# Layer 0's first two gate/value pairs computed from x times gain, before the shift is known, in a two-layer decoder kernel

## The chip, the cores and the metric

The kernel runs on one core of a Trainium2 chip. The number that counts is the device time of one launch in microseconds; the median of 3 runs of the kernel before is 2507.43 us (2504.96 to 2507.67).

Engines are named as in the profile: PE is TensorE (matrix products; PEld its weight loads), DVE VectorE, ACT ScalarE, POOL GpSimd, SP SyncE, which only issues DMAs here (a trailing q, as in ACTq, is an engine's issue queue). "bank" is one of the 8 PSUM banks of 128x512 float32.

## What is computed

```
for l in range(2):                                  # DEPTH
    mod = silu(c) @ w_ada[l] + b_ada[l]             # 9 * 1024 values: shift, scale, gate of three sub-layers
    h = rmsnorm(x, norm_ffn1[l]) * (1 + sc1) + sh1  # x is 512 x 1024
    x = x + 0.5 * g1 * (silu(h @ Wgate) * (h @ Wvalue)) @ Wdown      # 1024 -> 2 x 2816 -> 1024
    h = rmsnorm(x, norm_mix[l]) * (1 + sc2) + sh2
    x = x + g2 * mixer(h)                           # retention and windowed attention, gated, w_out
    h = rmsnorm(x, norm_ffn2[l]) * (1 + sc3) + sh3
    x = x + 0.5 * g3 * (silu(h @ Wgate) * (h @ Wvalue)) @ Wdown
out = rmsnorm(x, final_norm)
```

All is float32. With gain = norm weight * (1 + scale) and r the reciprocal root mean square of a token, h @ W equals r * ((x * gain) @ W) + shift @ W. So a product can start on x * gain alone; r is multiplied in afterwards, and shift @ W, one number per output column, is added.

## The kernel before

Activations lie transposed: 8 tiles of 128 model dimensions by 512 tokens (KT = 8, T = 512, P = 128). Each float32 operand is split into a high part (fp32r) and a low remainder, and each product is three matmuls (L1600 hi*hi, L1601 lo*hi, L1602 hi*lo). A "unit" is 128 output columns: 8 tiles of 3 matmuls for an up projection, 11 of 3 for a down projection. A "pair" is two units: one gate column block (unit 0, `pA[0]`) and its value block (unit 1, `pA[1]`), or two output blocks. Units of the same number share one raw buffer, one `w_hi` and one `w_lo` buffer, so for each unit SP loads 512 KB (`load`, L365) once DVE has split the unit in that buffer before it, ACT writes the high part (`split_weights`, L568) once PE has finished that earlier unit, DVE writes the low part (L943, a subtraction), and only then PE may start. The order on each engine is the written order; semaphores join them (`lo_ready` counts low parts, `unit_done` units, `bank_free` freed banks).

A feed-forward network runs in two halves: 11 up pairs (`up`: ACT Silu of the gate bank L681, DVE product with the value bank L1121, ACT high part L688, DVE low part L1124), then 4 down pairs, whose results DVE adds to x (L1097).

The modulation vector is computed on the side, 256 columns at a time, in "jobs" (`ada_sum_job`, L953 to L967): ACT issues the two loads of a job's 1 MB, DVE makes 8 multiply-adds of 128x256, one 32x32 transpose and one reduction. In ffn1 one job follows each up and down pair in DVE's order. `fold_jobs` (L1653) on PE sums the parts of a group of jobs once `ada_part_done` has counted them, and `ada_store` (L974) on DVE adds the bias. Job groups are GATE, MIX, REST and NEXT (the next layer's shift and scale).

Before the first pair of layer 0, shift and scale of ffn1 are computed from 16 blocks of 512 KB (`first_block`): PE multiplies a part of the columns (`first_rows`, L1561), DVE the others (`first_sum`, L1270 and L1273). x is transposed on PE (L1575). DVE and ACT then make tile after tile: x * r (L1286), times gain (L781), plus shift, high part (L785), low part (L1336). Layer 1 and the other norms already use the other way (`first_pairs` on ACT and DVE, `deferred_pairs` on PE): scaled x first, GpSimd sums shift times weight out of the raw buffer (`shift_products`, L489 to L497), PE sums that over its rows (`shift_sums`, L1632).

## Time and profile before

| what | value |
|---|---|
| median of 3 runs | 2507.43 us (2504.96 to 2507.67) |
| the profiled execution's own time | 2506.7 us |
| its span on the core | 2504.9 us |
| PE busy | 2472.0 us, 99% |
| DVE, ACT, POOL busy | 1501.5 us, 872.2 us, 210.3 us |
| DMA | 307.31 MB, mean 123 GB/s |
| chain that ended last, by engine | PE 94%, DVE 2%, issue 1%, ACT 1% |

The profile is one execution. Its span starts 1.8 us short of the time of that execution; every time of a row is counted from the start of the span. A busy time of PE counts a matmul until its last row has left, so consecutive rows overlap: the pitch of their starts is what a matmul costs. In an idle note, "[0.16 <-DVE sb_w_lo L943]" says that the engine was idle 0.16 us and which instruction it waited for.

### The profile page before, as it was taken

Reading aid. Unit: us, or ns where it says so; the run is one execution under the profiler, and the core shown is the slowest. Engines: PE = TensorE matmul, PEld = TensorE weight load, DVE = VectorE, ACT = ScalarE, POOL = GpSimd, SP = SyncE. Lnnn points to the kernel's source line nnn. Section 1 sums busy time; section 2 is a strip of 40 time slices with the busy share of each in tenths; the row PEclk is TensorE's granted clock in tenths of the full one; section 3 lists DMA queues with packets and bytes.
Section 4 is the critical chain, followed back from the end, with each engine's and each line's share of the span. In section 5 each row is a group of like instructions: output and inputs, shape, how many; then the busy total and the mean of one; then the engine's idle time right before and its main releaser. Section 6 shows DMA issues by size and latency. Waiting matters only on the chain.

```text
span 2504.9 us, 35621 instructions
## 1 busy us (share of the span) xinstructions
PE 2472.0 (99%) x11468; PEld 2012.8 (80%) x11468; DVE 1501.5 (60%) x2297; ACT 872.2 (35%) x1326; POOL 210.3 (8%) x151
## 2 busy tenths in 40 slices
PE   7999999999999999999999999999999999999998
PEld 5888888877788878888878888887777888788887
DVE  5677778677643477533467677877775435633332
ACT  3222333555423343222332223345553323331332
POOL 0013002000000040000140000210100002200001
PEclk9999999999999999999999999999999999999999
DMA  6665664222134336433336656532222343333332
GB/s 246 195 188 173 187 181 148 86 66 59 53 92 133 94 91 196 140 101 100 102 97 198 186 174 197 165 116 78 59 59 65 95 134 93 88 106 88 96 105 80
DMA packets 488916, 307.31 MB, mean 123 GB/s; under 512 B 9000, under 2 KB 480376, under 8 KB 488184
## 3 DMA queue, kind: packets, MB, share of 16 engines
q1 hardware_dynamic: 420816, 238.73, 32.2%
q10 hardware_dynamic: 68008, 67.48, 8.5%
q8 instruction: 41, 0.67, 0.1%
q14 instruction: 51, 0.42, 0.1%
HBM read 299.89 MB, written 6.29 MB: 122 GB/s over the span
## 4 chain that ended last, share of the span: by engine, by line
PE 94%; DVE 2%; issue 1%; ACT 1%; DMA 0%; DVEq 0%; SPq 0%; ACTq 0%
PE ps_proj L1600 28%; PE ps_proj L1602 28%; PE ps_proj L1601 28%; PE ps_mid L1870 1%; PE ps_mid L1766 1%; PE ps_o L1787 1%; PE ps_mid L1817 1%; PE ps_mid L1819 1%; PE ps_mid L1818 1%; PE ps_mid L1774 1%; PE ps_mid L1862 1%; DMA sb_scratch<-in_x 0%; DVE sb_scratch L1017 0%; PE ps_small L1593 0%; ACT sb_w_hi L568 0%
## 5 line engine op out<-in xcount | busy, mean ns | idle before, releaser
L1600 PE MATMUL ps_proj<-sb_a_hi,sb_w_hi 128*128 128x512 f32 x1908 | 745.5, 391 | 2.2 <-ACT sb_scratch L681 1.7
L1602 PE MATMUL ps_proj<-sb_a_hi,sb_w_lo 128*128 128x512 f32 x1908 | 742.8, 389 | 0.0
L1601 PE MATMUL ps_proj<-sb_a_lo,sb_w_hi 128*128 128x512 f32 x1908 | 742.8, 389 | 0.0
L568 ACT ACTIVATE sb_w_hi<-sb_raw 128x1024 fp32r<-128x1024 f32 (+1 forms) x388 | 430.9, 1110 | 849.1 <-PE ps_proj L1602 816.2
L943 DVE TENSOR_TENSOR sb_w_lo<-sb_raw,sb_w_hi 128x1024 fp32r<-128x1024 f32 (+1 forms) x388 | 514.1, 1325 | 323.2 <-ACT sb_w_hi L568 315.4
L1600 PE MATMUL ps_proj<-sb_h_hi,sb_w_hi 128*128 128x512 f32 x1212 | 480.1, 396 | 6.0 <-DVE sb_h_lo L1025 3.9
L1602 PE MATMUL ps_proj<-sb_h_hi,sb_w_lo 128*128 128x512 f32 x1212 | 472.4, 390 | 0.0
L1601 PE MATMUL ps_proj<-sb_h_lo,sb_w_hi 128*128 128x512 f32 x1212 | 472.2, 390 | 0.0
L1600 PEld LDWEIGHTS ps_proj<-sb_a_hi,sb_w_hi 128*128 128x128 f32 x1908 | 358.5, 188 | 78.7 <-ACT sb_scratch L681 3.0
L1602 PEld LDWEIGHTS ps_proj<-sb_a_hi,sb_w_lo 128*128 128x128 f32 x1908 | 358.4, 188 | 74.6
L1601 PEld LDWEIGHTS ps_proj<-sb_a_lo,sb_w_hi 128*128 128x128 f32 x1908 | 358.6, 188 | 74.3 <-issue 0.5
L1600 PEld LDWEIGHTS ps_proj<-sb_h_hi,sb_w_hi 128*128 128x128 f32 x1212 | 227.6, 188 | 66.4 <-issue 14.0
L1602 PEld LDWEIGHTS ps_proj<-sb_h_hi,sb_w_lo 128*128 128x128 f32 x1212 | 227.6, 188 | 48.5
L1601 PEld LDWEIGHTS ps_proj<-sb_h_lo,sb_w_hi 128*128 128x128 f32 x1212 | 227.7, 188 | 45.3
L955 DVE SCALAR_TENSOR_TENSOR sb_scratch<-sb_scratch,sb_c_act 128x256 f32<-128x256 f32 x448 | 223.7, 499 | 16.1
L471 POOL TENSOR_TENSOR sb_scratch<-sb_scratch 128x512 f32<-128x512 f32 x36 | 61.3, 1702 | 1567.1 <-ACT sb_scratch L579 1567.1
L1097 DVE SCALAR_TENSOR_TENSOR sb_x_or_values<-ps_proj,sb_half_gate,sb_x_or_values 128x512 f32 (+1 forms) x80 | 60.0, 750 | 198.5 <-PE ps_proj L1602 196.9
L1121 DVE TENSOR_TENSOR sb_scratch<-sb_scratch,ps_proj 128x512 f32<-128x512 f32 x82 | 56.4, 688 | 173.7 <-PE ps_proj L1602 173.5
L681 ACT ACTIVATE sb_scratch<-ps_proj 128x512 f32<-128x512 f32 x82 | 49.0, 598 | 303.8 <-PE ps_proj L1602 303.8
L752 ACT ACTIVATE sb_scratch<-sb_scratch,sb_small 128x256 f32<-128x256 f32 x128 | 63.1, 495 | 0.0
L1010 DVE SCALAR_TENSOR_TENSOR sb_h_lo<-sb_x_or_values,sb_gain,sb_h_hi (+1 forms) x40 | 58.7, 1467 | 5.6 <-ACT sb_h_hi L614 5.0
L1124 DVE TENSOR_TENSOR sb_a_lo<-sb_scratch,sb_a_hi 128x512 f32 (+1 forms) x82 | 56.1, 684 | 0.0
(210 smaller groups left out, 1824.6 us busy)
## 6 DMA issues: line engine op xcount, KB each, us to landing
sb_raw<-in_ffn_w_up SPq DMA_DIRECT2D x176, 512.0 KB, 3.8
sb_scratch<-in_w_ada ACTq DMA_DIRECT2D x128, 512.0 KB, 4.2
sb_raw<-in_w_in SPq DMA_DIRECT2D x100, 512.0 KB, 3.8
sb_raw<-in_ffn_w_down SPq DMA_DIRECT2D x64, 704.0 KB, 4.5
sb_raw<-in_w_branch_swa SPq DMA_DIRECT2D x16, 512.0 KB, 3.6
sb_raw<-in_w_branch_ret SPq DMA_DIRECT2D x16, 512.0 KB, 3.6
sb_raw<-in_w_out SPq DMA_DIRECT2D x16, 512.0 KB, 3.5
sb_scratch<-in_w_ada SPq DMA_DIRECT2D x10, 512.0 KB, 7.4
```

What stands on the lines that cost most here:

```text
L471: pool.tensor_tensor(square_sum, square_sum, squares[:, k % 2, :], ALU.add).then_inc(sq_used, 1)
L568: act.activation(Whi[s][:, 0:n], raw[s][:, 0:n], ACT.Copy).then_inc(hi_ready, 1)
L752: last = act.activation(p, p, ACT.Exp, bias=neg_m[w][:, n:n + 1], scale=HD ** -0.5, accum_out=row_sum[w][:, n:n + 1])
L943: dve.tensor_tensor(Wlo[s][:, 0:n], raw[s][:, 0:n], Whi[s][:, 0:n].bitcast(F), ALU.subtract).then_inc(lo_ready, 1)
L955: ins = dve.scalar_tensor_tensor(ada_acc, ada_raw[s][:, k % 4, :], col, ada_acc, ALU.mult, ALU.add)
L1010: dve.scalar_tensor_tensor(Hlo[:, k, :], XV[:, k, :], gain[:, bass.ds(k, 1)], Hhi[:, k, :].bitcast(F), ALU.mult, ALU.subtract).then_inc(gx ...
L1097: dve.scalar_tensor_tensor(XV[:, m, :], pA[s][:, :], half_gate[:, bass.ds(m, 1)], XV[:, m, :], ALU.mult, ALU.add).then_inc(bank_free[s], 1)
L1121: dve.tensor_tensor(work, side, pA[1][:, :], ALU.mult).then_inc(bank_free[1], 1)
L1124: dve.tensor_tensor(Alo[:, i, :], work, Ahi[:, i, :].bitcast(F), ALU.subtract).then_inc(act_lo, 1)
L1600: pe.matmul(bank, Whi[s][:, w], hi, start=first, stop=False)
L1601: pe.matmul(bank, Whi[s][:, w], lo, start=False, stop=False)
L1602: return pe.matmul(bank, Wlo[s][:, w], hi, start=False, stop=last)
```

## The change

- Head of layer 0. x is loaded in 4 blocks of 128 tokens, each between two scale blocks, and transposed block by block. DVE no longer multiplies x by r there: ACT and DVE split x * gain (`scaled_hi`, `scaled_lo`) as soon as the scale is known. Pairs 0 and 1 run on that. The shift blocks (now wholly on DVE, 128x1024 each) are summed meanwhile. Pair 2 is the first on normalised and shifted tiles, by tile; pair 3 follows. The four pairs are written out ahead of the loop over layers.
- The shift columns of pair 0 are 16 one-column products on PE among the products of pair 2 (`kept_columns`), those of pair 1 are made by GpSimd after the last normalised tile and summed by PE in the middle of pair 3 (`kept_sums`). Both read the weights of these units from a second copy in SBUF, loaded again (`keep`, 4 loads of 512 KB).
- Jobs. Layer 0's job 0 comes after pair 3 instead of after pair 1, and each further job after one up pair later than before. In layer 1 too the jobs run one pair later. Half 0 of ffn1 now has 13 jobs instead of 14, and the last job of a layer runs after pair 2 of ffn2. GATE is 8 jobs instead of 9, MIX 16 instead of 15. The REST group is folded in ffn2 and not in the mixer's first pair; NEXT is folded after half 0's down pairs of ffn2, and its first job, which stood in half 1, runs with the others.

```diff
-SCALE_PE, SHIFT_PE, FIRST_BUFS = 6, 4, 9
-ACT_COPIES, FIRST_AHEAD = (5, 6, 7), 3
-HALF_JOBS = (JOBS - FIRST_JOBS) // 2
-GATE_JOBS, MIX_JOBS = HALF - 2, HALF + 4
+SCALE_PE, FIRST_BUFS = 4, 9
+HALF_JOBS = HALF + KT // 2 - 2
+GATE_JOBS, MIX_JOBS = HALF - 3, HALF + 5
...
+            for n in range(2 * KT):                                          # SP
+                if n < TT:
+                    sp.dma_start(xtok[:, n, :], x[0, P * n:P * (n + 1), :]).then_inc(x_in[n], 16)
+                if n == KT - 1:
+                    load(0, 0, up_v[0][0, 0, 0])
+                first_block(n)
+                if n == KT - 1:
+                    load(0, 1, up_v[0][0, 1, 0])
+                if n == KT + TT - 1:
+                    for s in range(2):
+                        load(1, s, up_v[0][0, s, 1])
...
+            keep(0)
+            for s in range(2):
+                load(2, s, up_v[0][0, s, 2])
+            keep(1)
...
+            pool.wait_ge(split_lo, KT)                                       # POOL
+            for s in range(2):
+                pool.wait_ge(kept_in[1][s], 16)
+                st.mark(pool.tensor_tensor(shift_tmp..., kept[1][s]..., shift, ALU.mult))
+                for n in (UP_UNIT // 2, UP_UNIT // 4):
+                    st.mark(pool.tensor_tensor(shift_tmp[:, 0:n], shift_tmp[:, 0:n], shift_tmp[:, n:2 * n], ALU.add))
+                pool.tensor_tensor(shift_acc[2 + s], shift_tmp[:, 0:P], shift_tmp[:, P:2 * P], ALU.add).then_inc(shift_made, 1)
...
+                hi(2, 3, 4, 5, 6, 7)                                         # ACT, end of the head
+                gate(0, 0)
+                split_weights(3, 0, UP_UNIT)
+                rest(0, 0)
+                split_weights(3, 1, UP_UNIT)
+                act.wait_ge(unit_done, 2 * 2 + 3)
+                act.wait_ge(bank_free[1], 2)
+                act.activation(side, pair_banks[2][0], ACT.Silu).then_inc(bank_free[0], 1)
+                rest(2, 1)
+                gate(1, 2)
+                rest(1, 2)
...
+            for k in range(KT):                                              # DVE
+                dve.wait_ge(gain_ready, 1)
+                scaled_lo(0, k)
+                if k == TT - 1:
+                    split_weights(0, 1, UP_UNIT)
...
+                def gate(p, turn):
+                    dve.wait_ge(shift_ps, p + 1)
+                    dve.tensor_copy(shift_col[:, 2 * p:2 * p + 2], first_sums[p]).then_inc(shift_cols, 1)
+                    dve.wait_ge(unit_done, 2 * p + 3)
+                    dve.wait_ge(act_lo, turn + 1)
+                    dve.tensor_tensor(work, pair_banks[p][0][:, :], rstd_row, ALU.mult).then_inc(scaled, 1)
...
+                lo(7)
+                gate(0, 0)
+                split_weights(3, 0, UP_UNIT)
+                value(0, 0)
+                rest(0, 0)
+                split_weights(3, 1, UP_UNIT)
...
+                dve.tensor_tensor(work, side, pair_banks[2][1], ALU.mult).then_inc(bank_free[1], 1)
+                rest(2, 1)
+                gate(1, 2)
+                value(1, 2)
+                rest(1, 2)
+                ada_sum_job(0, FIRST_JOBS, 0)
...
-                rest = FIRST_JOBS + GATE_JOBS + MIX_JOBS                     # DVE, mixer's first pair
-                ada_store(fold_no(l, REST_FOLD), rest, JOBS - rest, MOD_TILES * l + 2 * rest)
...
+                idle(pair_banks[1][0], 3)                                    # PE
+                for s in range(2):
+                    unit(0, 0, s, h_tile, waits={} if s else {k: (gx_lo, k + 1) for k in range(KT)})
+                unit(1, 1, 0, h_tile, ..., after={SPREAD_AT: lambda: spread_rstd(0, pO, 0).then_inc(rb_ready, 1)})
+                unit(1, 1, 1, h_tile, ..., after={KT - 2: shift_columns})
+                idle(pair_banks[2][0], 2)
...
+                unit(3, 3, 0, tile, freed=1)
+                unit(3, 3, 1, tile, freed=1, after={2: kept_sums})
```

In the three places below, rows name the line of the kernel they belong to, the operation, what is written and read, and the shape.

DVE, layer 0, from the splits of pair 3's weights to the first split of pair 4's, before. L943 is the low part of a weight unit (the digit is its buffer), L1121 and L1124 the product and low part of an up pair, L953 to L967 a job.

```order
L943 TENSOR_TENSOR sb_w_lo0<-sb_raw0,sb_w_hi0 128x1024
...
L953 TENSOR_SCALAR sb_scratch<-sb_scratch,sb_c_act 128x256
...
L967 TENSOR_REDUCE sb_scratch<-sb_scratch 128x8
L1144 UNCONDITIONAL_BRANCH
...
L1121 TENSOR_TENSOR sb_scratch<-sb_scratch,ps_proj1 128x512
...
L943 TENSOR_TENSOR sb_w_lo1<-sb_raw1,sb_w_hi1 128x1024
L1124 TENSOR_TENSOR sb_a_lo<-sb_scratch,sb_a_hi 128x512
```

The same stretch after the change, where L1009 is the low part of a weight unit, L1437 the product of pair 2, L1390 to L1405 the late work of pair 1, L1019 to L1033 the job, and L1206 the branch over layer 1's first pairs, behind which the first split of pair 4 stands.

```order
L1009 TENSOR_TENSOR sb_w_lo1<-sb_raw1,sb_w_hi1 128x1024
L1437 TENSOR_TENSOR sb_scratch<-sb_scratch,ps_mid 128x512
...
L1390 COPY sb_small<-ps_o 128x2
L1393 TENSOR_TENSOR sb_scratch<-ps_mid,sb_scratch 128x512
L1399 TENSOR_TENSOR sb_scratch<-ps_mid,sb_scratch 128x512
L1401 SCALAR_TENSOR_TENSOR sb_scratch<-sb_scratch,sb_small 128x512
L1405 TENSOR_TENSOR sb_a_lo<-sb_scratch,sb_a_hi 128x512
L1019 TENSOR_SCALAR sb_scratch<-sb_scratch,sb_c_act 128x256
L1021 SCALAR_TENSOR_TENSOR sb_scratch<-sb_scratch,sb_c_act 128x256 x7
L1031 STREAM_TRANSPOSE sb_scratch<-sb_scratch 128x256
L1033 TENSOR_REDUCE sb_ada_part<-sb_scratch 128x8
L1446 TENSOR_SCALAR sb_sinks<-sb_sinks 128x32
```

Between the last split of pair 3 and the first of pair 4 stood one up pair's two operations and one job; now the products of pairs 2 and 1 and a job stand there.

PE, layer 0, unit 1 of pair 3 and what follows, after the change: L1706 to L1708 are the three matmuls of a product (on `ps_proj1`), L1792 the two sums of `kept_sums`, L1928 and L1863 the entry of the loop over layers, behind which the skipped pairs of layer 1 and then pair 4 stand. Before, no such sum stood among the products of layer 0's pair 3.

```order
L1706 MATMUL ps_proj1<-sb_a_hi,sb_w_hi1 128x512
L1707 MATMUL ps_proj1<-sb_a_lo,sb_w_hi1 128x512
L1708 MATMUL ps_proj1<-sb_a_hi,sb_w_lo1 128x512
L1792 MATMUL ps_o<-sb_consts,sb_scratch 128x1 x2
L1706 MATMUL ps_proj1<-sb_a_hi,sb_w_hi1 128x512
...
L1928 UNCONDITIONAL_BRANCH
L1863 COMPARE_AND_BRANCH
```

What moved: the sums come after three of the eight tiles of that unit, and DVE's late work of pair 1 waits for them.

DVE, the mixer's first pair in both layers, before: L1017 scales a tile, L1025 is its low part, L1353 scales a unit's result, L974 is `ada_store` of the REST group (four rows of 32 partitions).

```order
L1025 SCALAR_TENSOR_TENSOR sb_h_lo<-sb_scratch,sb_mod,sb_h_hi 128x512
L1352 REGISTER_ALU
L1353 TENSOR_TENSOR sb_scratch<-ps_proj,sb_scratch 128x512
L974 ISA
L974 TENSOR_TENSOR sb_mod<-ps_mid,sb_vector_cols 32x8
...
L1017 SCALAR_TENSOR_TENSOR sb_scratch<-sb_scratch,sb_gain,sb_x_or_values 128x512
L1024 REGISTER_ALU
L1025 SCALAR_TENSOR_TENSOR sb_h_lo<-sb_scratch,sb_mod,sb_h_hi 128x512
```

After the change the four L974 rows and their registers are gone from this place; they stand at the end of ffn2's first up half.

## Rows read from the trace of the kernel before

**Rows 1.** Page, section 1, busy time, and section 2, PE's granted clock in 40 slices

```profile
PE 2472.0 (99%) x11468; PEld 2012.8 (80%) x11468; DVE 1501.5 (60%) x2297; ACT 872.2 (35%) x1326; POOL 210.3 (8%) x151
PEclk9999999999999999999999999999999999999999
```

**Rows 2.** PE's waits over the span: us in total, times, longest

```profile
PE ps_proj L1600 <- DVE sb_h_lo L1025: 3.9, 8, 0.8
PE ps_mid L1817 <- DVE sb_h_lo L1025: 2.0, 2, 1.0
```

**Rows 3.** Timeline of PE: start us, duration us, engine, line, operation, [idle before]

```profile
15.16 1.09 PE L1575 MATMUL ps_proj<-sb_consts,sb_scratch 128*128 128x128 f32 x8 [2.99 <-DMA sb_scratch<-in_x]
...
28.71 3.68 PE L1561 MATMUL ps_mid<-sb_scratch,sb_c_act 128*128 128x512 f32 x8
...
45.34 1.42 PE L1600 MATMUL ps_proj<-sb_a_hi,sb_w_hi 128*128 128x512 f32 x1
...
58.39 0.49 PE L1600 MATMUL ps_proj<-sb_a_hi,sb_w_hi 128*128 128x512 f32 x1 [0.34 <-DVE sb_w_lo L943]
...
91.47 0.49 PE L1600 MATMUL ps_proj<-sb_a_hi,sb_w_hi 128*128 128x512 f32 x1 [0.16 <-DVE sb_w_lo L943]
```

**Rows 4.** Timeline of ACT, head: weight splits that waited for their load

```profile
23.43 1.06 ACT L568 ACTIVATE sb_w_hi<-sb_raw 128x1024 fp32r<-128x1024 f32 x1 [2.15 <-DMA sb_raw<-in_ffn_w_up]
25.16 1.06 ACT L568 ACTIVATE sb_w_hi<-sb_raw 128x1024 fp32r<-128x1024 f32 x1 [0.68 <-DMA sb_raw<-in_ffn_w_up]
```

**Rows 5.** Timeline of DVE, head: operations of the scale columns and shift sum

```profile
24.06 0.48 DVE L1273 SCALAR_TENSOR_TENSOR sb_pos_i<-sb_consts,sb_c_act,sb_pos_i 128x256 f32<-128x256 f32 x1
...
29.61 0.95 DVE L1294 TENSOR_REDUCE sb_scratch<-sb_scratch 128x6 f32<-128x768 f32 x1
...
31.94 0.75 DVE L1273 SCALAR_TENSOR_TENSOR sb_scratch<-sb_scratch,sb_c_act 128x512 f32<-128x512 f32 x1
```

**Rows 6.** Groups of DVE and ACT by form: count, busy us, mean ns

```profile
L943 DVE TENSOR_TENSOR sb_w_lo<-sb_raw,sb_w_hi 128x1024 fp32r<-128x1024 f32 x324 | 407.9, 1259 | 285.6 <-ACT sb_w_hi L568 277.8 <-DVE sb_scratch L1219 0.5
L1121 DVE TENSOR_TENSOR sb_scratch<-sb_scratch,ps_proj 128x512 f32<-128x512 f32 x82 | 56.4, 688 | 173.7 <-PE ps_proj L1602 173.5
L1017 DVE SCALAR_TENSOR_TENSOR sb_scratch<-sb_scratch,sb_gain,sb_x_or_values 128x512 f32<-128x512 f32 x30 | 22.9, 764 | 0.1
L688 ACT ACTIVATE sb_a_hi<-sb_scratch 128x512 f32 x64 | 40.5, 633 | 1.1
L614 ACT ACTIVATE sb_h_hi<-sb_x_or_values,sb_gain 128x512 fp32r<-128x512 f32 x20 | 14.2, 710 | 5.0 <-DVE sb_gain L1004 5.0
```

**Rows 7.** Timeline of PE, layer 0's mixer: 8 one-column sums of two passes

```profile
410.10 1.84 PE L1593 MATMUL ps_small<-sb_consts,sb_scratch 128*128 128x1 f32 x16
```

**Rows 8.** Timeline of POOL, layer 0's ffn2: one unit's shift products

```profile
913.91 2.10 POOL L489 TENSOR_TENSOR sb_scratch<-sb_raw,sb_mod 128x1024 f32<-128x1024 f32 x1 [0.20 <-POOL sb_scratch L497]
916.18 1.51 POOL L494 TENSOR_TENSOR sb_scratch<-sb_scratch 128x512 f32<-128x512 f32 x1 [0.18 <-POOL sb_scratch L489]
917.88 1.50 POOL L494 TENSOR_TENSOR sb_scratch<-sb_scratch 128x256 f32<-128x256 f32 x1 [0.18 <-POOL sb_scratch L494]
919.87 0.56 POOL L497 TENSOR_TENSOR sb_scratch<-sb_scratch 128x128 f32<-128x128 f32 x1 [0.49 <-POOL sb_scratch L494]
```

**Rows 9.** Timeline of DVE in the same stretch

```profile
916.48 2.30 DVE L943 TENSOR_TENSOR sb_w_lo<-sb_raw,sb_w_hi 128x1024 fp32r<-128x1024 f32 x1
...
918.78 0.68 DVE L1041 TENSOR_TENSOR sb_scratch<-ps_proj,sb_scratch 128x512 f32<-128x512 f32 x1
```

**Rows 10.** Timeline of DVE, head: job 0 from first to last operation

```profile
77.26 0.34 DVE L953 TENSOR_SCALAR sb_scratch<-sb_scratch,sb_c_act 128x256 f32<-128x256 f32 x1
...
81.77 0.42 DVE L967 TENSOR_REDUCE sb_scratch<-sb_scratch 128x8 f32<-128x256 f32 x1
```

**Rows 11.** Stretches: length, busy time of PE, PEld, DVE, ACT, POOL, granted clock, DMA

```profile
39.00:42.00 3.00, 1.03 (x6) 1.03 (x6) 2.41 (x4) 0.00 (x0) 0.00 (x0) 0.86 0.39 82
42.00:45.00 3.00, 3.00 (x7) 1.71 (x7) 2.16 (x5) 2.06 (x4) 0.00 (x0) 0.50 0.93 377
45.00:48.00 3.00, 3.00 (x7) 1.83 (x6) 3.00 (x6) 2.94 (x5) 0.00 (x0) 0.50 0.50 160
48.00:51.00 3.00, 3.00 (x15) 2.48 (x14) 1.24 (x3) 0.00 (x0) 0.00 (x0) 1.00 0.92 269
```

**Rows 12.** Timeline, layer 0's ffn1, down pairs of half 1: PE's fold, DVE's job

```profile
355.04 0.38 PE L1653 MATMUL ps_mid<-sb_scratch,sb_consts 128*128 128x120 f32 x2
...
355.82 0.42 DVE L967 TENSOR_REDUCE sb_scratch<-sb_scratch 128x8 f32<-128x256 f32 x1
```

**Rows 13.** Timeline, mixer's first pair of layer 0: DVE's store, PE's second tile

```profile
422.09 0.68 DVE L974 TENSOR_TENSOR sb_mod<-ps_mid,sb_vector_cols 32x8 f32<-32x8 f32 x4
...
424.27 0.50 PE L1817 MATMUL ps_mid<-sb_w_hi,sb_h_hi 128*128 128x512 f32 x1 [0.99 <-DVE sb_h_lo L1025]
```

386 lines of the change are left out of this document (219 added, 167 removed).

## Prediction

> **What bounds the kernel now.** I read the page's busy times and PE's granted clock first. PE is busy 2472.0 of 2504.9 us at the full clock [rows 1], so only its holes or its work can move the time. The list of PE's waits comes second: its entries inside the layers are a few us (3.9 and 2.0 us are the largest two [rows 2]), so the stages behind the head have little to give. The timeline of PE comes third. Its first product starts at 45.3 us, pair 1 at 58.4 us, pair 4 at 91.5 us [rows 3]; from pair 1 to pair 4 that is 33.1 us for three pairs, 11.0 us each, which is 0.227 us per matmul (48 to a pair) with a hole of some tenths at two borders. So the head, up to 45.3 us, is what the change can earn from, and I follow it to the point where both kernels do the same again: the start of pair 4, 91.5 us before.
>
> **When pair 0 starts.** The bytes ahead of pair 0's second unit are the same as before (x, 8 scale blocks, 2 units), so it lands at 25.2 us as before; the last scale block and the first unit change places, and I put the block at the 23.4 us at which that unit landed [rows 4]. DVE then does the low part of unit 0 (1.2 us [rows 6], to 24.5), a copy (0.4), the last scale sum of 512 columns (0.75 us [rows 5], to 25.6), product with the identity and reduction of 512 columns (0.7 us each, scaled from 0.95 us for 768 [rows 5]) and three small adds: the gain is there at 27.4 us. ACT needs 0.71 us for the first tile, DVE 0.75 us [rows 6]. First product: 29.0 us. Before it PE has four filler matmuls, the last three at 0.9 us each at the full clock [rows 3] (the eight passes at 28.71 are four blocks), which end there too. Bounds: 27 us if the block lands 2 us earlier, 31.7 us if PE has the lower clock by then and its fillers take double.
>
> **PE from there to the middle of pair 3.** Pairs 0 to 2 and 11 of pair 3's 16 tile steps are 3.7 pairs of 10.9 us, 40.2 us. Added: spreading r 0.8, 8 + 16 one-column products at 0.21 us (8 take 1.7 us of pitch [rows 7]) 5.1, two filler matmuls 1.7, the two sums of pair 1's shift 0.4. Waits: 1.0 in pair 0, since DVE makes the tiles at 0.67 us each, PE's own pace, and stops once for a 1.2 us split; 2.0 at pair 2, where each tile costs DVE two operations of 0.75 us; 0.8 at pair 3, whose unit 0 can be split only when PE has left unit 0 of pair 2 (ACT 1.06 us [rows 4], then DVE). Sum 52.0 us: PE ends the sums of `kept_sums` at 81.0 us, and without any wait would end pair 3 at 84.4 us. Up to here it is 7 us ahead of before.
>
> GpSimd does not decide this by itself. Its four operations take 2.1 + 1.5 + 1.5 + 0.6 us and four gaps, 6.2 us per unit [rows 8], 12 us for both; the last tile is there at 65.5 us, so it ends near 78 us, 2 us before PE asks.
>
> **The wait that replaces the head's.** Pair 4's unit 0 waits for its low part, and DVE has all this before it: copy 0.15, gate of pair 1 times r 0.69, ACT's Silu 0.7, value times r 0.69, product 0.75, ACT's high part 0.63, low part 0.69 [rows 6], then job 0, 4.9 us from 77.26 to 82.19 [rows 10], sinks and loop entry 0.6, the split 1.2, and 0.2 of handing over. That is 11.2 us in a row from 81.0, no part of which can begin before PE's sums: pair 4 starts at 92.2 us. PE has 3.4 us of work for these 11.2, and stands still for 7.8. Before, job 0 lay under pair 2, where DVE had nothing else [rows 10]; now it is on the path. So pair 4 starts 0.7 us later than before, and the whole gain of the head is spent there. The later pairs have 8.7 us of DVE work (split 1.2 twice, 0.69 twice, a job 4.9) against 10.9 of PE, so the lag doesn't grow.
>
> **What the hole does to the clock.** Before, PE is idle 2 us near 39 to 41 us after a thin stretch, its granted clock falls within 39 to 42 and is 0.50, that is 1.2 GHz, until 48, though PE is busy all the time from 42 [rows 11]. 7.8 us of idleness is more than any hole in this trace before its last product. If the clock falls as it did there, the products behind run at half speed for up to (1 - 0.86) * 2 * 3 + 6 = 6.8 us, a loss of up to 3.4 us. Lower bound 0: the 2.99 us hole at 12 to 15 us left the clock full [rows 3]. I take 2.5, near the upper end, since this hole is nearer in kind to the one that cost. The Trainium skill, "TensorE: Matmul & The Clock Gate", Part 1, speaks against the change here: the slower clock is the default and only activity lifts it. By that rule the loss is certain; by the 2.99 us hole alone the sum would be 2.5 us less.
>
> **DVE beside GpSimd.** The low part of a unit takes 1.26 us on average [rows 6] and 2.30 us beside GpSimd, while a product that reads PSUM keeps 0.68 us [rows 9]. I charged pair 3's first split so (2.3 us); without it pair 4 would start 0.8 us earlier. The Trainium skill, "GPSIMD Engine Reference", section 1, says that the SBUF interfaces are shared with VectorE, with contention for instructions that have two SBUF inputs; the trace agrees. By a rule that slowed every DVE operation, the sum would be about 1 us more.
>
> **The rest of the program.** MIX is folded after the first unit of half 1's down pairs. Before, it needed 24 jobs of 25 done; now it needs 24 of 24, the last being the job of up pair 10. PE's fold starts at 355.04, that job ends at 356.24 [rows 12]: a new wait of 1.2 us in each layer, 2.4. REST: the store of 0.7 us leaves DVE ahead of the tile that PE waits 0.99 us for in the mixer's first pair [rows 13]: 0.7 less in each layer, 1.4. The folds cost PE the same where they now stand, and the job moved to ffn2 lies under products of 10.9 us. Bounds of this part: -1.4 (no new wait) to +2.4; I take +1.0, since both come from rows of the very places. The 2 MB loaded twice and SP's stop at `load(1, 1)` behind unit 1's split (32 us) put the last shift block at 41 us, and DVE needs it at 48, so I take 0, up to 1 us if the queue lands as slowly as its 9 us at worst.
>
> **Sum.** +0.7 + 2.5 + 1.0 = +4.2 us. The profiled execution took 2506.7 us, so 2510.9 for its like; the median of the runs is 0.7 above it, which gives 2511.6 us. Least: start at 27 (-2), no contention (-0.8), clock full (0), rest -1.4, so 0.7 - 4.2 = -3.5. Most: lower clock at pair 0 (+2.7), columns and GpSimd dearer (+1.1), clock 3.4, rest 2.0, so +9.9.
>
> **The rivals.**
> - The hole at pair 4 doesn't lower the clock: +1.7, 2509.1 us. For it the 2.99 us hole, against it the length. 13%.
> - The clock is already low when pair 0 starts, since PE has less to do in the head (512 instead of 768 columns per scale block): +2.7 on top, +6.9, 2514.3 us. For it the fall at 41 us in a similar thin stretch [rows 11], against it that 15 to 33 us stayed full. 20%.
> - The other side: DVE's chain isn't the bound, because pair 1's late work or the job finishes under pair 3. Then pair 4 starts at 84.4, 7.1 us early, and the clock holds: -7.1 + 1.0 = -6.1, 2501.3 us, faster. It decides if the chain behind the sums is under 3.4 us instead of 11.2. For it: DVE has a quarter of the time idle in the head; against it: the written order. 8%.
> - A weight unit or shift block lands so late that PE waits for loads in pairs 1 to 3: each us late is a us, from about 7 us behind my times on; with 2 us, 2513.6 us. 9%.
> - The forecast as summed: 50%.
>
> **Range and chances.** What a measurement of this kernel can tell from no change is about 0.2%, 5 us. The forecast lies at +4.2 with some 2 us of spread, so a third of its 50 lies beyond +5; with nearly all of the low-clock rival and half of the late loads that is 41% slower. Faster is the third rival, 7%; the same 52%. The range takes in both clock cases and the lower end of the sum to -3 : 2504.5 to 2516.5.
>
> **What the new profile would show.** PE's first product at 29 us; about 16 us for pair 2; one PE wait of 7 to 8 us for DVE's low part at the start of pair 4, near 84 to 92 us, the longest of the span; granted clock at 0.50 behind it for 3 to 7 us; the job directly ahead of that split on DVE; waits of 1.2 us before the MIX folds near 356 and 1582 us. I am wrong if pair 4 starts before 89 us, if the hole is under 4 us, or if the clock stays full.

## The result, and the profile after

The changed kernel takes 2514.71 us (median of 11 runs, 2513.42 to 2519.49) against 2506.87 us of the kernel before (11 runs beside them): ratio 1.0032, 95% interval 1.0023 to 1.0040, slower by some 8 us. The profiled execution took 2514.69 us, its span is 2512.9 us. The page's busy times, which answer to [rows 1]:

```profile
PE 2473.7 (98%) x11490; PEld 2014.3 (80%) x11490; DVE 1514.4 (60%) x2303; ACT 878.1 (35%) x1332; POOL 222.3 (9%) x159
```

PE is busy 1.7 us longer; the other 6 us of the longer span are holes. PE's waits over the span, against [rows 2]:

```profile
PE ps_proj L1706 <- DVE sb_w_lo L1009: 8.5, 1, 8.5
PE ps_proj L1706 <- DVE sb_h_lo L1091: 4.1, 8, 0.8
PE ps_mid L1758 <- DVE sb_ada_part L1033: 2.2, 2, 1.1
PE ps_mid L1950 <- DVE sb_h_lo L1091: 0.5, 2, 0.3
```

One wait of 8.5 us is new and the longest; two of 1.1 us at a fold are new; the two in the mixer went from 2.0 to 0.5 us. Where the first stands, in PE's timeline of the head (the first products of pairs 0, 2 and 4, and the sums of pair 1), against [rows 3]:

```profile
23.58 1.12 PE L1667 MATMUL ps_mid<-sb_scratch,sb_c_act 128*128 128x512 f32 x2 [1.94 <-DMA sb_scratch<-in_w_ada]
24.55 1.73 PE L1777 MATMUL ps_mid<-sb_x_or_values,sb_consts 128*128 128x512 f32 x2
26.07 1.71 PE L1771 MATMUL ps_small<-sb_consts,sb_scratch 128*128 128x1 f32 x8
27.64 4.76 PE L1777 MATMUL ps_mid<-sb_x_or_values,sb_consts 128*128 128x512 f32 x6
31.83 0.80 PE L1706 MATMUL ps_proj<-sb_h_hi,sb_w_hi 128*128 128x512 f32 x1
...
59.00 0.47 PE L1706 MATMUL ps_mid<-sb_a_hi,sb_w_hi 128*128 128x512 f32 x1 [0.37 <-DVE sb_a_lo L1091]
...
83.00 0.50 PE L1792 MATMUL ps_o<-sb_consts,sb_scratch 128*128 128x1 f32 x4
...
95.51 0.79 PE L1706 MATMUL ps_proj<-sb_a_hi,sb_w_hi 128*128 128x512 f32 x1 [8.47 <-DVE sb_w_lo L1009]
```

Pair 0 starts 13.5 us earlier than before (45.34), pair 4 starts 4.0 us later (91.47). The six passes of three filler products take 4.76 us, 0.8 us each (a filler is a product with the identity whose result nobody reads; each takes two passes). The stretches of the same profile show the clock (columns as in [rows 11]):

```profile
24.00:27.00 3.00, 3.00 (x10) 1.60 (x8) 2.75 (x5) 1.06 (x1) 0.00 (x0) 0.62 1.04 394
27.00:30.00 3.00, 3.00 (x7) 1.79 (x8) 1.55 (x6) 1.79 (x3) 0.00 (x0) 0.50 1.04 385
30.00:33.00 3.00, 3.00 (x8) 1.50 (x7) 3.00 (x5) 3.00 (x6) 0.00 (x0) 0.74 0.40 97
```

```profile
87.00:90.00 3.00, 0.05 (x1) 0.00 (x0) 2.53 (x6) 1.84 (x3) 0.00 (x0) 0.93 0.02 5
90.00:93.00 3.00, 0.00 (x0) 0.00 (x0) 2.77 (x7) 0.40 (x1) 0.00 (x0) 0.50 0.56 171
96.00:99.00 3.00, 3.00 (x8) 2.33 (x8) 2.90 (x5) 0.63 (x1) 0.00 (x0) 0.50 0.61 181
99.00:102.00 3.00, 3.00 (x13) 2.38 (x12) 2.81 (x6) 0.00 (x0) 0.00 (x0) 0.86 0.62 174
```

It is at 0.50, 1.2 GHz, twice: behind the wait of 1.94 us, until pair 0's first product, and in the hole before pair 4, until 99.5 us. What DVE does while PE stands still (timeline, from PE's sums of pair 1 to pair 4's first split):

```profile
83.61 0.69 DVE L1393 TENSOR_TENSOR sb_scratch<-ps_mid,sb_scratch 128x512 f32<-128x512 f32 x1
85.15 0.69 DVE L1399 TENSOR_TENSOR sb_scratch<-ps_mid,sb_scratch 128x512 f32<-128x512 f32 x1 [0.85 <-ACT sb_scratch L825]
85.88 0.75 DVE L1401 SCALAR_TENSOR_TENSOR sb_scratch<-sb_scratch,sb_small 128x512 f32<-128x512 f32 x1
87.33 0.69 DVE L1405 TENSOR_TENSOR sb_a_lo<-sb_scratch,sb_a_hi 128x512 fp32r<-128x512 f32 x1 [0.70 <-ACT sb_a_hi L829]
87.94 0.35 DVE L1019 TENSOR_SCALAR sb_scratch<-sb_scratch,sb_c_act 128x256 f32<-128x256 f32 x1
88.32 3.61 DVE L1021 SCALAR_TENSOR_TENSOR sb_scratch<-sb_scratch,sb_c_act 128x256 f32<-128x256 f32 x7
...
92.77 0.17 DVE L1446 TENSOR_SCALAR sb_sinks<-sb_sinks 128x32 f32<-128x32 f32 x1
94.11 1.22 DVE L1009 TENSOR_TENSOR sb_w_lo<-sb_raw,sb_w_hi 128x1024 fp32r<-128x1024 f32 x1 [1.16 <-ACT sb_w_hi L608]
```

Late work, job, sinks, the loop's entry, split: 12.0 us from the end of PE's sums (83.50) to pair 4. Its gaps are two waits for ACT inside pair 1's late work (0.85 and 0.70 us) and 1.16 us before the split. The profile puts this last one down to ACT, but ACT's high part of that unit had ended at 88.9 us; what stands there in DVE's order is the entry of the loop over layers. In run 8, where the split is no longer there, a gap of 1.20 us stands behind the same sinks and the profile puts it to "issue".

Followed through the program by PE's start times after minus before: pair 0 -13.5, pair 4 +4.0, the mixer's first pair +6.4 (424.27 to 430.63), layer 1 +6.8, its mixer +7.4 (1650.37 to 1657.75), end of the span +8.0 us.

### The profile page after: what moved, and what is told of

Same layout as the page of the kernel before. It is cut to its first block, busy times and chain, and to the rows that moved or that the text cites. A ratio compares the mean times of both kernels' runs of the same rounds, so it can differ in the third digit from the quotient of the medians.

```text
span 2512.9 us, 35648 instructions
## 1 busy us (share of the span) xinstructions
PE 2473.7 (98%) x11490; PEld 2014.3 (80%) x11490; DVE 1514.4 (60%) x2303; ACT 878.1 (35%) x1332; POOL 222.3 (9%) x159
## 4 chain that ended last, share of the span: by engine, by line
PE 91%; DVE 2%; issue 1%; ACT 1%; DVEq 0%; ACTq 0%
PE ps_proj L1706 27%; PE ps_proj L1708 27%; PE ps_proj L1707 27%; PE ps_mid L2003 1%; PE ps_mid L1903 1%; PE ps_o L1924 1%; PE ps_mid L1950 1%; PE ps_mid L1952 1%; PE ps_mid L1951 1%; PE ps_mid L1911 1%; PE ps_mid L1995 1%; ACT sb_w_hi L608 0%; DVE sb_scratch L1083 0%; PE ps_small L1699 0%; DVE sb_w_lo L1009 0%
## 5 line engine op out<-in xcount | busy, mean ns | idle before, releaser
L1706 PE MATMUL ps_proj<-sb_a_hi,sb_w_hi 128*128 128x512 f32 x1878 | 734.0, 391 | 10.2 <-DVE sb_w_lo L1009 8.5
L1708 PE MATMUL ps_proj<-sb_a_hi,sb_w_lo 128*128 128x512 f32 x1878 | 731.5, 390 | 0.0
L1707 PE MATMUL ps_proj<-sb_a_lo,sb_w_hi 128*128 128x512 f32 x1878 | 731.4, 389 | 0.0
L1009 DVE TENSOR_TENSOR sb_w_lo<-sb_raw,sb_w_hi 128x1024 fp32r<-128x1024 f32 (+1 forms) x388 | 514.2, 1325 | 319.2 <-ACT sb_w_hi L608 306.3
L1706 PE MATMUL ps_proj<-sb_h_hi,sb_w_hi 128*128 128x512 f32 x1210 | 479.7, 396 | 6.1 <-DVE sb_h_lo L1091 4.1
L1708 PE MATMUL ps_proj<-sb_h_hi,sb_w_lo 128*128 128x512 f32 x1210 | 471.6, 390 | 0.0
L1706 PEld LDWEIGHTS ps_proj<-sb_a_hi,sb_w_hi 128*128 128x128 f32 x1878 | 353.0, 188 | 85.5 <-issue 8.9
L1708 PEld LDWEIGHTS ps_proj<-sb_a_hi,sb_w_lo 128*128 128x128 f32 x1878 | 352.9, 188 | 73.8
L1707 PEld LDWEIGHTS ps_proj<-sb_a_lo,sb_w_hi 128*128 128x128 f32 x1878 | 353.2, 188 | 72.6
L1706 PEld LDWEIGHTS ps_proj<-sb_h_hi,sb_w_hi 128*128 128x128 f32 x1210 | 227.2, 188 | 66.9 <-issue 14.1
L1708 PEld LDWEIGHTS ps_proj<-sb_h_hi,sb_w_lo 128*128 128x128 f32 x1210 | 227.1, 188 | 48.5
L1076 DVE SCALAR_TENSOR_TENSOR sb_h_lo<-sb_x_or_values,sb_gain,sb_h_hi 128x512 fp32r<-128x512 f32 (+1 forms) x48 | 64.2, 1347 | 6.4 <-ACT sb_h_hi L649 6.2
L775 ACT ACTIVATE sb_scratch<-ps_proj 32x512 f32<-32x512 f32 (+1 forms) x48 | 28.4, 591 | 78.9 <-PE ps_proj L1708 78.6
```

Of the source, the lines that this page charges most:

```text
L1009: dve.tensor_tensor(Wlo[s][:, 0:n], raw[s][:, 0:n], Whi[s][:, 0:n].bitcast(F), ALU.subtract).then_inc(lo_ready, 1)
L1076: dve.scalar_tensor_tensor(Hlo[:, k, :], XV[:, k, :], gain[:, bass.ds(k, 1)], Hhi[:, k, :].bitcast(F), ALU.mult, ALU.subtract).then_inc(gx ...
L1706: pe.matmul(bank, Whi[s][:, w], hi, start=first, stop=False)
L1707: pe.matmul(bank, Whi[s][:, w], lo, start=False, stop=False)
L1708: return pe.matmul(bank, Wlo[s][:, w], hi, start=False, stop=last)
```

## The experiments

Each was timed against the kernel before; the "changed kernel" below is the one of this document, 2514.7 us.

**1. Most of job 0 left out.** Seven multiply-adds of job 0 are gone from DVE.

```diff
-                ada_sum_job(0, FIRST_JOBS, 0)
+                ins = dve.tensor_scalar(ada_acc, ada_raw[0][:, 0, :], c_act[:, 0:1], None, ALU.mult)
+                ...   # semaphores raised as the job does
+                dve.transpose(ada_turned, ada_acc).then_inc(ada_turn, 1)
+                dve.reduce_sum(ada_part[:, 0:8], ...).then_inc(ada_part_done, 1)
```

> Changed kernel; of job 0 only the first multiply, the transpose and the reduction are left on DVE, the seven multiply-adds (3.6 us) are left out, so 256 columns of the modulation vector are wrong. Theory A (DVE's row of work between the two sums of pair 1 and pair 4's first split sets pair 4's start): pair 4 starts 3.6 us earlier, at 91.9 instead of 95.5 us, the hole is 4.9 instead of 8.5 us, and the time falls by 3.6 us to 2511.1 us, or by up to 5.5 us to 2509.2 us if the shorter hole leaves the clock full. Rival B (the hole ends with the landing of pair 4's weights or with ACT's split): pair 4 starts within 0.5 us of 95.5, and the time stays at 2514.7 us within 1 us.

Measured: 2509.64 us (11 runs), ratio 1.0011 (1.0002 to 1.0020), 5.1 us less. PE's hole in its timeline:

```profile
96.64 0.79 PE L1715 MATMUL ps_proj<-sb_a_hi,sb_w_hi 128*128 128x512 f32 x1 [5.06 <-DVE sb_w_lo L1009]
```

The hole is 3.4 us shorter, as theory A has it; rival B falls. Pair 4 starts no earlier in this execution (2516.56 us, one of the two longest of the eleven), since pair 2 ran at the lower clock in it and PE came to the sums at 87.5 instead of 83.0 us; from the start of the sums to pair 4 it is 9.1 us instead of 12.5. The median gained 1.5 us more than the 3.6 of the job. That isn't the clock held at the shorter hole, as far as this one profile goes: the granted clock fell to 0.50 there too (96 to 102 us).

**2. Filler ahead of the last scale block.**

```diff
+                if k == KT - 1:
+                    pe.wait_ge(xt_act, 2 * TT)
+                    for _ in range(2):
+                        pe.matmul(pair_banks[1][0], ident, XV[:, 0, :], start=True, stop=True)
                 first_rows(k, scale_rows)
```

> Changed kernel; two filler products (four passes of 0.43 us at the full clock) are put on PE ahead of the last scale block, into the hole of 1.94 us that ends at 23.6 us. Theory A (that hole lets the clock fall to 0.50 at 24.9 us, and the six passes of filler behind the scale columns, 4.8 us at half speed, hold pair 0 back): the clock stays at 1.00 from 21 to 33 us, pair 0 starts at 29.9 us instead of 31.8, pair 4 at 93.5, and the time falls by 2 us to 2512.7 us. Rival B (the clock falls for what lies before, the thin work from 3 to 20 us, or DVE's pair 2 work absorbs the earlier start): the clock is 0.50 as before, or pair 4 starts at 95.5 all the same, and the time stays at 2514.7 us.

Measured: 2517.49 us (6 runs, 2515.36 to 2521.19), ratio 1.0037 (1.0025 to 1.0049): not faster; 2.8 us more by the medians, but the intervals of the two ratios overlap. In the stretches of its profile, one of the two longest executions of the six:

```profile
27.00:30.00 3.00, 2.92 (x9) 1.38 (x8) 2.09 (x6) 2.65 (x5) 0.00 (x0) 1.00 1.03 383
...
60.00:63.00 3.00, 2.29 (x11) 2.03 (x11) 2.93 (x6) 1.44 (x2) 0.00 (x0) 0.74 0.97 286
63.00:66.00 3.00, 3.00 (x9) 2.45 (x9) 2.96 (x5) 1.44 (x2) 0.00 (x0) 0.50 0.03 8
72.00:75.00 3.00, 3.00 (x8) 2.32 (x9) 0.77 (x2) 0.72 (x1) 2.82 (x2) 0.50 0.00 0
```

As theory A has it, the clock stays full in the head and pair 0 starts at 29.09 us, 2.7 us earlier. Neither theory had what follows: pair 2 starts 2.0 us earlier, at 57.0, the clock falls at 61 us, where PE waits for DVE's tiles, and stays at 0.50 to 75 us; PE reaches the sums of pair 1 at 87.1 instead of 83.0 us. This is theory C of the runs below. The filler isn't needed for it: runs 1, 4, 6 and 11 have none there, and the clock fell in pair 2 too.

**3. The MIX fold inside the second unit.**

```diff
-                        down(0, lambda: fold_jobs(fold_no(l, MIX_FOLD), ...))
+                        down(0, inside={4: lambda: fold_jobs(fold_no(l, MIX_FOLD), ...)})
```

> Changed kernel; the MIX group is folded after the fifth of the eleven steps of the first down pair's second unit in half 1, 3.4 us later than before in PE's order. Theory A (the fold waits 1.1 us for the last job in each layer, and DVE has slack behind it): both waits of 1.1 us go, nothing takes their place, and the time falls by 2.2 us to 2512.5 us. Rival B (gain and first tiles of the mixer are then late, since the store on DVE stands ahead of its splits): the waits are there again at the next down unit, and the time is 2514.7 us or up to 2 us more.

Measured: 2512.44 us (11 runs), ratio 1.0019 (1.0009 to 1.0028), 2.3 us less. The two waits of 1.1 us are gone from the list of PE's waits, and none of that size took their place. Theory A holds.

**4. GpSimd's shift products left out.**

```diff
-                st.mark(pool.tensor_tensor(shift_tmp..., kept[1][s]..., shift, ALU.mult))
-                ...   # and the three additions
+                pool.memset(shift_acc[2 + s], 0.0).then_inc(shift_made, 1)
```

> Changed kernel; GpSimd's shift products for pair 1 (12.5 us from 68.8 on) are left out and its sums set to zero, so pair 1's shift is left out of the result. Theory A (GpSimd makes DVE's work beside it longer, the split of 1.73 us instead of 1.22, the product of 1.67 instead of 0.75, but DVE then waits 0.78 us for PE's sums at 83.0 anyway): DVE's operations are short again, it waits 2.5 us for the sums, pair 4 starts at 95.5 us within 0.3, and the time stays at 2514.7 us. Rival B (my forecast's charge: contention delays pair 3's splits and so PE): pair 4 starts 0.8 us or more earlier and the time falls to 2513.9 us or below.

Measured: 2514.10 us (11 runs), ratio 1.0029 (1.0019 to 1.0038). DVE in its timeline:

```profile
78.93 0.75 DVE L1393 SCALAR_TENSOR_TENSOR sb_scratch<-sb_scratch,sb_small 128x512 f32<-128x512 f32 x1
...
81.33 1.23 DVE L1001 TENSOR_TENSOR sb_w_lo<-sb_raw,sb_w_hi 128x1024 fp32r<-128x1024 f32 x1 [0.26 <-ACT sb_w_hi L600]
...
86.51 0.16 DVE L1382 COPY sb_small<-ps_o 128x2 f32<-128x2 f32 x1 [1.96 <-PE ps_o L1784]
```

In the changed kernel the same two took 1.67 and 1.73 us beside GpSimd. Without it they are short again, and DVE waits longer for PE's sums. From the sums to pair 4 it is 12.5 us in both (85.97 to 98.50 here, in an execution with the lower clock in pair 2). The 0.6 us between the medians can't be told from nothing. Theory A holds: the contention is there and costs no time that these runs can show.

The same profile shows something else. Its head is that of the changed kernel, with the same wait for the last scale block, but the clock did not fall behind it (PE's timeline, then the stretch):

```profile
23.75 1.12 PE L1659 MATMUL ps_mid<-sb_scratch,sb_c_act 128*128 128x512 f32 x2 [1.94 <-DMA sb_scratch<-in_w_ada]
```

```profile
24.00:27.00 3.00, 3.00 (x13) 1.62 (x13) 2.75 (x5) 1.06 (x1) 0.00 (x0) 1.00 1.05 393
```

Pair 0 starts at 29.54 us here, against 31.83 in the changed kernel's profile.

**5. The same work in another order.** ACT's order follows.

```diff
                 gate(0, 0)                                  # DVE
-                split_weights(3, 0, UP_UNIT)
                 value(0, 0)
                 rest(0, 0)
-                split_weights(3, 1, UP_UNIT)
+                split_weights(3, 0, UP_UNIT)
                 ...   # three waits
                 dve.tensor_tensor(work, side, pair_banks[2][1], ALU.mult).then_inc(bank_free[1], 1)
+                split_weights(3, 1, UP_UNIT)
                 rest(2, 1)
+                ada_sum_job(0, FIRST_JOBS, 0)
                 gate(1, 2)
                 value(1, 2)
                 rest(1, 2)
-                ada_sum_job(0, FIRST_JOBS, 0)
```

> Changed kernel; the same work in another order. DVE does pair 0's value and low part before the first split of pair 3, pair 2's product before the second, and job 0 before the late work of pair 1; ACT's order follows. Theory A (DVE's row of work is what ends the hole; it can be begun earlier, since DVE idles 3.9 us before pair 3's split): DVE has done pair 2's low part by about 79.5 us, job 0 by 84.5, the row behind it is 4.4 + 1.35 + 1.2 us, pair 4 starts at 91.7 us instead of 95.5, the hole is 4.8 us, and the time is 2510.9 us, or up to 1.9 less if the clock holds. Rival B (beside GpSimd the moved operations and the job take twice as long, and pair 3's splits come late): pair 3 starts later than 75.7 us, the job takes over 7 us, and less than 1.5 us is gained.

Measured: 2511.05 us (11 runs), ratio 1.0017 (1.0008 to 1.0026), 3.7 us less. PE's hole:

```profile
92.42 0.79 PE L1706 MATMUL ps_proj<-sb_a_hi,sb_w_hi 128*128 128x512 f32 x1 [5.39 <-DVE sb_w_lo L1009]
```

Theory A gave 91.7 us and a hole of 4.8: it holds in place and nearly in size.

**6. Pair 4's first split ahead of the loop**, on top of 5.

```diff
                 gate(1, 2)
+                split_weights(4, 0, UP_UNIT)
                 value(1, 2)
...
-                        with st.loop(3, HALF - 1, 0) as i:
+                        else:
+                            up(3, UP_UNIT, job, False)      # ffn1; layer 1 splits behind up(2)
+                        with st.loop(3 if f else 4, HALF - 1, 0) as i:
```

> As the run with the other order, and pair 4's first split is taken out of the loop over layers and put between gate and value of pair 1 (in layer 1 behind pair 2's work). Theory A: pair 4 then waits only for the bank that ACT's Silu of pair 3 frees, which waits for pair 1's value: job 0 to 84.5, gate and split 2.0, value 1.5, two ACT operations 1.2, so pair 4 starts at 89.2 us, the hole is 2.3 us and leaves the clock full; the time is 2514.7 - 6.3 - 1.9 = 2506.5 us. Rival B (the entry of the loop, 1.2 us, and ACT's order stand between all the same): pair 4 starts after 91 us and the time is above 2509 us.

Measured: 2507.53 us (11 runs), ratio 1.0006 (0.9997 to 1.0015), 7.2 us less. Its profile has the lower clock in pair 2 again (65 to 75 us), so pair 4 starts at 92.42 us, but only 5.0 us behind the sums, and its hole is

```profile
92.42 0.50 PE L1714 MATMUL ps_proj<-sb_a_hi,sb_w_hi 128*128 128x512 f32 x1 [0.98 <-ACT sb_scratch L716]
```

It ends with ACT's Silu, as theory A has it. Its 0.98 us are the hole of an execution with the lower clock in pair 2; run 8, with the same order and the full clock in pair 2, has 2.76 us there, near the 2.3 of the theory. By the medians of runs 5 and 6 the hole was the largest part of the loss.

**7. Fillers in pair 2.**

```diff
+                    if k < 2:
+                        w = 256 + 128 * k
+                        pe.matmul(pair_banks[2][1][:, 0:w], ident, XV[:, 0, 0:w], start=True, stop=True)
                     if 1 <= k <= 4:
                         sums = kept_columns(...)
```

> Changed kernel; two filler products of 256 and 384 columns (0.43 and 0.64 us at the full clock) are put behind the first two steps of pair 2, where PE waits 0.43 and 0.71 us for DVE. Theory C (PE's thin stretch at 57 to 63 us lets the clock fall in some executions, as in the profiles of three of the four runs so far, which makes pair 2 some 4 us longer and the scatter of the times): the clock is 1.00 from 57 to 87 us, the median is 2514.5 us, and no time is above 2517 us. Rival D (the clock falls for another reason, as the DMA load of 300 GB/s from 36 to 57 us): the profile or several times still show it, some times are 2517 to 2520 us, and the median is 2514.7 to 2515.7 us.

Measured: 2512.97 us (8 runs, 2511.61 to 2517.64), ratio 1.0026 (1.0016 to 1.0037). The clock is 1.00 from 27 to 87 us:

```profile
60.00:63.00 3.00, 2.93 (x21) 2.45 (x19) 2.93 (x6) 1.40 (x2) 0.00 (x0) 1.00 0.94 298
66.00:69.00 3.00, 3.00 (x19) 2.61 (x18) 1.95 (x4) 0.31 (x1) 1.48 (x1) 1.00 0.00 0
```

PE was busy 1.93 of 3 us in the first stretch of the changed kernel, 2.29 in run 2, and is 2.93 here. One time of eight is still above 2517, where theory C had none and the changed kernel three of eleven; that decides nothing. What speaks for theory C comes from all the profiles together: the table below run 12.

**8. All edits together.**

> Changed kernel with all edits together: the order and the split ahead of the loop, the filler ahead of the last scale block, the two fillers in pair 2, and the MIX fold after the fifth step. Theories A and C together: the clock is 1.00 from 21 to 90 us, pair 0 starts at 29.1 us, pair 2 at 57.0, pair 4 at 86.5 behind a hole of about 2.3 us, no wait for the MIX folds; the time is 2514.7 - 2.7 - 6.3 - 1.9 - 2.2 = 2501.6 us, 5 us under the kernel before. If C is wrong, pair 2's clock falls now and then, and the median is 2504 to 2506 us; if only the separate gains hold that lie in different places, it is between these.

Measured: 2504.86 us (11 runs, 2501.90 to 2507.19), ratio 0.9991 (0.9982 to 1.0000). Pair 0 starts at 29.1, pair 4 at 88.08 us behind 2.76 us. The time is 3.3 us above what the sum of gains gave. The hole:

```profile
88.08 0.80 PE L1718 MATMUL ps_proj<-sb_a_hi,sb_w_hi 128*128 128x512 f32 x1 [2.76 <-ACT sb_scratch L716]
```

The clock falls in it (0.63 from 87 to 90 us), and once more at the passage from layer 0 to layer 1 (0.76 from 1266 to 1272 us).

**9. Fillers in the hole before pair 4.**

```diff
                 unit(3, 3, 1, tile, freed=1, after={2: kept_sums})
+                pe.wait_ge(bank_free[0], 3)
+                idle(pair_banks[2][0], 9)
```

> Changed kernel; nine filler products (7.7 us at the full clock) are put on PE between pair 3 and pair 4, into the hole of 8.5 us. Theory A (the hole lets the clock fall to 0.50, and nine products of pair 4 take 0.43 instead of 0.23 us each): the clock stays at 1.00 through pair 4's start, pair 4 starts at 95.5 us as before, and the time falls by 2.0 us to 2512.7 us. Rival B (the fall belongs to the power state of the whole head and comes anyway, or the fillers hold pair 4 back): the clock falls elsewhere in the first 110 us and the time stays at 2514.7 us.

Measured: 2519.32 us (5 runs, 2516.87 to 2519.88), ratio 1.0048 (1.0034 to 1.0062), slower than the changed kernel by the medians, with intervals that just overlap. The clock is full at pair 4, which starts at 94.50 us, and a job near 392 us starts its last operation 3.0 us earlier than in the changed kernel (391.62 against 394.62). Of these, 1.0 us was there when pair 4 started (pair 0 had started at 30.06 us), which leaves the 2.0 of theory A for the clock: it holds, as far as the place goes. The loss comes later, at the first product of layer 1 (timeline, then the stretches):

```profile
1274.36 0.79 PE L1706 MATMUL ps_proj<-sb_h_hi,sb_w_hi 128*128 128x512 f32 x1 [4.45 <-DVE sb_h_lo L1076]
```

```profile
1272.00:1278.00 6.00, 3.64 (x9) 2.88 (x10) 1.56 (x2) 0.14 (x1) 0.00 (x0) 0.55 0.32 93
1278.00:1284.00 6.00, 6.00 (x24) 5.42 (x23) 1.82 (x12) 0.00 (x0) 0.00 (x0) 0.50 0.01 3
```

The hole between the layers is 4.45 us instead of 1.80, and behind it PE runs at half speed until 1286 us. Why the hole grew is not known. The profile names DVE's low part L1076, but that can't be the cause: in the changed kernel the same operation ran from 1275.86 us on, and PE had started layer 1 at 1274.72, before it. One profile shows the hole; that all five times lie above 2516.8 us fits a loss in each execution, but doesn't place it.

**10. Job 0 in three parts, sums one step earlier, Silu before the copy**, on top of 8.

```diff
-                ada_sum_job(0, FIRST_JOBS, 0)               # DVE; the edits of ACT and PE are not shown
+                ada_sum_job(0, FIRST_JOBS, 0, 0, 5)
                 gate(1, 2)
                 split_weights(4, 0, UP_UNIT)
                 value(1, 2)
+                ada_sum_job(0, FIRST_JOBS, 0, 5, 6)
                 rest(1, 2)
+                ada_sum_job(0, FIRST_JOBS, 0, 6)
```

> The kernel with all edits, and four more in the row ahead of pair 4: job 0 is cut in three parts (five of its eight steps before the late work of pair 1, one between its value and its low part, the rest behind), PE takes the sums of pair 1 one step earlier, and ACT's Silu of pair 3 stands before its copy of pair 1. Theory A (only the row up to value and Silu bounds pair 4): DVE starts the late work at about 81.3 instead of 83.6 us, pair 4 starts at about 85.3 instead of 88.1 us, with up to 1 us of waiting at its second unit, and the clock stays full (another 1.2 us): 2504.9 - 2.8 - 1.2 + 1.0 = 2501.9 us. Rival B (what is taken off before pair 4 comes back before its second unit, since DVE's work there is the same 13 us): pair 4 starts earlier, its second unit at the same time as before, and the time is within 1 us of 2504.9.

Measured: 2503.93 us (11 runs, 2502.14 to 2506.69), ratio 0.9989 (0.9980 to 0.9998). There is no wait left at pair 4's first unit, which starts at 85.26 us; the next waits are those at its second unit and at pair 5:

```profile
91.54 0.50 PE L1730 MATMUL ps_proj<-sb_a_hi,sb_w_hi 128*128 128x512 f32 x1 [0.55 <-DVE sb_w_lo L1021]
98.24 0.49 PE L1730 MATMUL ps_proj<-sb_a_hi,sb_w_hi 128*128 128x512 f32 x1 [0.97 <-DVE sb_w_lo L1021]
```

The clock is 1.00 from 21 to 111 us. Between the layers it falls:

```profile
1260.00:1266.00 6.00, 4.13 (x15) 3.03 (x14) 3.26 (x3) 2.19 (x3) 2.68 (x4) 0.84 0.06 15
1266.00:1272.00 6.00, 6.00 (x23) 5.42 (x23) 1.96 (x12) 0.00 (x0) 0.00 (x0) 0.50 0.29 83
1272.00:1278.00 6.00, 6.00 (x26) 4.91 (x26) 1.28 (x1) 1.06 (x1) 5.04 (x4) 0.81 0.00 0
```

In place theory A was right: pair 4's first unit is 2.8 us and its second 3.6 us earlier than in run 8 (91.54 against 95.10). The time is where rival B had it: the gain of 0.9 us over run 8 can't be told from none. In the profiled execution, 18 us at a mean of 0.72 between the layers take up to 5 us back.

**11. One filler instead of three ahead of pair 0.**

```diff
-                idle(pair_banks[1][0], 3)
+                idle(pair_banks[1][0], 1)
```

> Changed kernel; one filler product instead of three behind the scale columns. Theory A (at the lower clock three of them take 4.8 us and end 2 us after the first tile's low part is there; that is what holds pair 0 at 31.8 us): pair 0 starts at about 29.9 us, but at the lower clock, and DVE's tiles come at 0.67 us each against 1.3 us that a step then takes, so part of the gain is lost again: 2513.5 us, between 2512.7 and 2514.7. Rival B (without the fillers the clock stays low for much longer, as PE is then less busy): the clock is still 0.50 at 36 us, pair 1 starts later than 43.2 us, and the time is above 2515 us.

Measured: 2515.84 us (6 runs, 2512.33 to 2518.72), ratio 1.0032 (1.0020 to 1.0044). Pair 0 starts at 30.03 us, but the clock, which was back at 1.00 from 27 us in this execution, falls again from 31 to 34 us and in pair 2. Nothing is won without two of the fillers. Nor does the run show that they hold pair 0 back: in runs 7 and 9, with all three and the clock likewise back at 1.00 from 27 us, pair 0 starts at 29.89 and 30.06 us. They can be what holds it only where the clock stays at 0.50 behind them, as in the changed kernel's profile, where the first tile's low part was there at 29.8 us. Which of the two theories is nearer stays open.

**12. The fillers of 2 and 7 together.**

> Changed kernel with the filler ahead of the last scale block and the two fillers in pair 2, nothing else. Theory C (the run with the first filler alone gained 2.7 us at pair 0 and lost more, since the clock then fell in pair 2's thin stretch): with both, the clock is 1.00 from 21 to 87 us, pair 0 starts at 29.1 us, pair 2 at 57.0, pair 4 at about 93.3, and the time is about 2.2 us under that of the changed kernel, 2512.5 us, 5 us under the 2517.5 of the first filler alone. Rival E (an earlier arrival lets the clock fall somewhere else, at the hole of 1.9 us between the layers for one): pair 4 starts early, the clock falls near 1270 us, and the time is 2514 to 2518 us.

Measured: 2514.83 us (11 runs, 2512.87 to 2515.63), ratio 1.0024 (1.0015 to 1.0033). The clock is full from 21 to 87 us, PE takes the sums of pair 1 at 81.23 instead of 83.00 us, and the mixer's first pair starts at 428.96 us, 1.7 us ahead of the changed kernel. In layer 1 it starts at 1658.69, 0.9 us behind it (1657.75): the clock falls between the layers (0.72 from 1278 to 1284 us), where it was 1.00 in the changed kernel. Rival E came true in that the early start of pair 4 brought nothing. PE also waits once more at this place, behind the hole that every profile has:

```profile
1273.23 0.49 PE L1710 MATMUL ps_proj<-sb_h_hi,sb_w_hi 128*128 128x512 f32 x1 [1.97 <-issue]
1276.20 0.39 PE L1712 MATMUL ps_proj<-sb_h_hi,sb_w_lo 128*128 128x512 f32 x1 [0.88 <-issue]
```

Where the granted clock was under 1.00 in the profiles, one execution each:

| kernel | head, 24 to 48 us | pair 2 | pair 4 | between the layers |
|---|---|---|---|---|
| before | yes | | | |
| changed, 3 | yes | | yes | |
| 5, 7 | yes | | yes | |
| 1, 11 | yes | yes | yes | |
| 2, 4 | | yes | yes | yes |
| 6 | yes | yes | | yes |
| 8, 12 | | | yes | yes |
| 9 | yes | | | yes |
| 10 | | | | yes |

Read by columns, the table says more than any one run. In the head the clock fell in eight of the nine profiles of changed kernels without the filler ahead of the last scale block, and in none of the four with it (2, 8, 10, 12). In pair 2 it fell in five of nine without fillers in it (1, 2, 4, 6, 11), and in none of the four with them (7, 8, 10, 12). So both fillers keep the clock where they stand. Pair 2 also goes with the scatter of the times: the five profiled executions in which it fell took 1.3 to 6.9 us more than the medians of their kernels, the eight in which it did not between 0.2 us less and 2.0 us more. Between the layers no edit and no arrival time sorts the profiles: the clock fell there with early starts of layer 1 (1263.02 us, run 10) and with late ones (1279.76 us, run 2), and stayed full with 1267.92 (before) and 1277.40 (run 11).

## Why the prediction was right or wrong

The measured 2514.7 us lies in the range, on the side forecast. The likeliest case gave 2511.6 us; the rival in which the clock is low when pair 0 starts gave 2514.3 us and had 20%. That rival came true, and eight of the nine profiles with this head show it, so 20% was too low; the mechanism was known. That its number comes within 0.4 us is partly luck: from the kernel before the rival gave +6.9 us, and measured were +7.8, with pair 4's start 0.6 us later than its +3.4, the clock behind the hole 0.6 us and the rest 0.2 us cheaper, and some 1.3 us by the end of the span that no term of the sum had; the kernel before itself took 2506.87 us beside this one instead of 2507.43.

**When pair 0 starts** is the step that was most off: 31.83 us instead of 29.0. Its DVE part was nearly right (the gain is there at 28.2 instead of 27.4 us, ACT's first tile starts at 28.21). The filler passes cost 0.8 instead of 0.46 us, as I had priced for the lower clock: my upper bound there was 31.7 us. What I took as evidence against a fall, the full clock from 15 to 33 us before, did not carry over: the changed head multiplies 512 instead of 768 columns per block on PE, and waits 1.94 us for the last one. This wait is what makes the fall likely, but it doesn't decide alone: filled, the clock held in four profiles of four (pair 0 at 29.1 to 29.4 us); unfilled, it held in run 4 as well, with pair 0 at 29.54 us. With the clock full, then, the step was 0.1 to 0.5 us off.

**PE to the middle of pair 3**: 52.0 us forecast, 51.5 measured (31.83 to the product at 83.36). Pair 2 took 16.2 us, as forecast 16. GpSimd ran from 68.8 to 81.1 us, 12.3 us for the 12 forecast, and ended 1.9 us before PE asked.

**The wait that replaces the head's**: right in mechanism, place and order. It was 8.47 us for 7.8, the row from the sums to pair 4 was 12.15 us (from PE's next product at 83.36 to 95.51) for 11.2. Of the 0.95 us too little, 0.7 is sinks and loop entry, 1.34 us (92.77 to 94.11) for my 0.6, a figure for which I had no row. Runs 1, 5, 6 and 10 each cut this row in another place and made PE's hole shorter, by about what they took off; with run 6 the hole is 1 us in its profile, 2.8 with a full clock in pair 2 (run 8), and most of the loss is gone.

**The clock at the hole**: forecast 2.5 us, measured 1.9: nine matmuls at a pitch of 0.43 us for 0.23 and the first 0.1. The clock was at 0.50 from 90 to 99 us. By the Trainium skill, "TensorE: Matmul & The Clock Gate", Part 1, for which the slower clock is the default, the fall was to be expected, and the trace agrees. All profiles say the same of this place: holes of 8.5, 5.4, 5.1 and 2.8 us before pair 4 were followed by 0.50, those of 1.0 us and less (runs 6 and 9) were not. But run 9, which took the fall away here, was no faster.

**DVE beside GpSimd**: the charge of 0.8 us was wrong, run 4. The split that I charged took 1.23 us, though it ran from 73.85 us on and GpSimd's second large product is shown from 73.99 to 76.84; why it wasn't stretched no run tells (the profile's times on GpSimd are rough). The operations that were stretched had DVE's wait for PE's sums behind them. The stretching of these is as the Trainium skill has it in "GPSIMD Engine Reference", section 1, for instructions with two SBUF inputs: 0.75 to 1.67 us, while a product that reads PSUM took 0.68 us as ever.

**The rest**: forecast +1.0 as the middle between bounds of -1.4 and +2.4, worked out +2.4 and -1.4; measured +2.2 and -1.4. The fold in layer 0 and the mixer's second tile:

```profile
362.34 0.49 PE L1758 MATMUL ps_mid<-sb_ada_part,sb_consts 128*128 128x128 f32 x2 [1.10 <-DVE sb_ada_part L1033]
```

```profile
430.63 0.50 PE L1950 MATMUL ps_mid<-sb_w_hi,sb_h_hi 128*128 128x512 f32 x1 [0.28 <-DVE sb_h_lo L1091]
```

The first is the wait of 1.2 us that [rows 12] gave, the second the 0.99 us of [rows 13] less 0.7; run 3 shows that the first pair of waits can be had back for nothing. A further 0.3 us in ffn2's first pairs of each layer I did not foresee and did not look into; it is part of the 1.3 us named above.

**What stays open.** Some executions of the changed kernel take 2517.6 to 2519.5 us. Profiles of other kernels with the same head show the clock at 0.50 in pair 2 with PE's sums of pair 1 up to 4.5 us later (87.53 instead of 83.00 in run 1), which would be that much; the profiled execution of the changed kernel itself did not have it. And what lets the clock fall between the layers no run here tells. The hole there is 1.76 to 2.06 us in all profiles but run 9's, and its length doesn't sort them: 1.94 us (before) and 2.06 (run 11) left the clock full, 1.86 to 1.91 (runs 2, 4, 6, 8, 10) did not.

## What to carry to other kernels

When work is taken off the front of a program, write down what the engine behind it must do in a row before the next shared step; here 12 us of DVE work waited for one small product, and PE's gain of 13.5 us was worth nothing until that row was cut. Put side work, as the job, where that engine waits for another, and take a loop's entry (1.2 us on DVE) out of such a row. And where an engine's waits of 1 to 2 us follow each other, price the clock at both levels before counting an earlier start as a gain, and judge a filler by the time of the whole program: the version with all edits (run 10) beats the kernel before by 0.1% and the changed kernel by 0.4%, where the sums of the single gains had given 0.5% over the changed kernel (2501.6 and 2501.9 us).

## What the runs showed of the hardware

Filler products kept the clock up where they stood, and that alone was seldom a gain: with the head filled it fell in pair 2 (run 2), with pair 2 filled too it fell between the layers (run 12), with the hole before pair 4 filled it fell between the layers as well, for longer (run 9). That the filling moved the fall is not shown: in runs 4 and 6, with neither place filled, the clock fell in pair 2 and between the layers too. Waits of 1.9 us were followed by 0.50 in some executions and by a full clock in others, in the head (run 3 against run 4) and between the layers (run 2 against run 1). Once down, the clock stayed at 0.50 for 4 us of busy PE behind the hole before pair 4 (changed kernel, 95.5 to 99.5 us), for about 10 us in pair 2 of runs 1 and 6 (65 to 75 us), and for about 12 us between the layers in run 9 (1274 to 1286 us). A fall costs a kernel that PE bounds up to 0.20 us per matmul of 128x512, from a pitch of 0.23 to one of 0.43 us.
